# A two-layer hybrid block on one Trainium2 core: expert weights in 16 KB runs, the gather between the products, and a tiled input stage

## The reference

```python
def expert_choice_ffn(x, w_router, w_gate_up, w_down):      # x (1, 512, 1024), 16 experts, width 1024
    cap = EC_CAPACITY_FACTOR * T // N_EXPERTS                # 64 rows for each expert
    aff = jax.nn.softmax(jnp.einsum('btd,de->bte', x, w_router), axis=-1)
    gate, idx = lax.top_k(jnp.swapaxes(aff, 1, 2), cap)
    xs = x[bidx, idx]
    hg, hu = jnp.split(jnp.einsum('becd,edf->becf', xs, w_gate_up), 2, axis=-1)
    ye = jnp.einsum('becf,efd->becd', jax.nn.silu(hg) * hu, w_down)
    return jnp.zeros_like(x).at[bidx, idx].add(ye * gate[..., None])

# end of second_block
mix = jnp.einsum('bsd,de->bse', merged, w_out[l])
x = layer_norm(DN_ALPHA * x + mix, ln1_g[l], ln1_b[l])
ffn = expert_choice_ffn(x, w_router[l], w_gate_up[l], w_down[l])
x = layer_norm(DN_ALPHA * x + ffn, ln2_g[l], ln2_b[l])
```

## Time and profile before

| | |
|---|---|
| median of 3 runs (lowest, highest) | 2690.31 us (2686.57, 2691.11) |
| profiled execution, its span | 2694.53 us, 2692.5 us |
| TensorE busy | 2480.3 us, 92% of the span |
| VectorE (DVE) busy | 1105.0 us, 41% |
| ScalarE (ACT) busy | 813.3 us, 30% |
| GpSimd (POOL) busy | 168.9 us, 6% |
| DMA | 400.42 MB, mean 149 GB/s |
| chain that ended last | PE 80%, DVE 8%, DMA 5%, ACT 4% |

### The profile page before, as it was taken

How to read it: one execution, slowest core, us unless ns; L and a number is a source line. 1 busy time by engine, 2 the same in 40 slices (tenths; PEclk the granted TensorE clock), 3 DMA queues, 4 the chain that set the end, 5 groups by cost and what they waited for, 6 DMA issues and landing times.

```text
span 2692.5 us, 31030 instructions
## 1 busy us (share of the span) xinstructions
PE 2480.3 (92%) x13300; PEld 1829.3 (68%) x13300; DVE 1105.0 (41%) x1487; ACT 813.3 (30%) x1289; POOL 168.9 (6%) x156
## 2 busy tenths in 40 slices
PE   6999999999998999979999999987999879999996
PEld 4787788877776777867778878854778744444442
DVE  4747465343433323254334472657433621111113
ACT  5434544232323313142233343335422200000000
POOL 0102021111110000000000010210000000000000
PEclk9999999999998999989999999989999879999998
DMA  4122213232314223231222332331321279999995
GB/s 134 55 75 79 86 42 106 75 110 83 105 63 156 94 102 112 80 137 63 94 94 85 106 131 94 110 90 44 110 94 60 105 314 409 409 409 409 409 409 205
DMA packets 153800, 400.42 MB, mean 149 GB/s; under 512 B 7232, under 2 KB 25024, under 8 KB 153536
## 3 DMA queue, kind: packets, MB, share of 16 engines
q1 hardware_dynamic: 149504, 383.76, 38.3%
q0 software_dynamic: 4160, 14.68, 1.6%
HBM read 384.53 MB, written 13.89 MB: 148 GB/s over the span
## 4 chain that ended last, share of the span: by engine, by line
PE 80%; DVE 8%; DMA 5%; ACT 4%; issue 2%; SPq 0%; ACTq 0%; DVEq 0%
PE banks L94 19%; PE banks L96 18%; PE banks L95 18%; PE banks L1925 4%; PE banks L1956 4%; DMA work<-w_down_in 2%; PE banks L1906 2%; PE banks L1983 2%; DMA ring<-w_down_in 2%; DVE ring_split L88 1%; PE banks L1540 1%; PE banks L1438 1%; ACT halves_split L83 1%; DVE const L2421 1%; PE banks L1444 1%
## 5 line engine op out<-in xcount | busy, mean ns | idle before, releaser
L94 PE MATMUL banks<-work_split,ring_split 128*128 128x512 f32 x1536 | 625.2, 407 | 35.4 <-DVE ring_split L88 21.2
L88 DVE TENSOR_TENSOR ring_split<-ring,halves_split 128x1024 fp32r<-128x1024 f32 x284 | 355.6, 1266 | 680.0 <-ACT halves_split L83 679.9
L95 PE MATMUL banks<-work_split,halves_split 128*128 128x512 f32 x1536 | 605.8, 394 | 0.0
L96 PE MATMUL banks<-activations_T_split,halves_split 128*128 128x512 f32 x1184 | 468.0, 395 | 0.0
L83 ACT ACTIVATE halves_split<-ring 128x1024 fp32r<-128x1024 f32 x284 | 294.8, 1052 | 311.9 <-PE banks L96 258.7
L94 PEld LDWEIGHTS banks<-work_split,ring_split 128*128 128x128 f32 x1536 | 293.3, 191 | 108.3 <-DVE ring_split L88 24.9
L95 PEld LDWEIGHTS banks<-work_split,halves_split 128*128 128x128 f32 x1536 | 293.7, 191 | 58.6 <-issue 1.0
L96 PE MATMUL banks<-ring_split,work_split 128*128 128x512 f32 (+1 forms) x736 | 286.2, 389 | 0.0
L95 PE MATMUL banks<-halves_split,work_split 128*128 128x512 f32 x672 | 264.9, 394 | 0.0
L96 PEld LDWEIGHTS banks<-activations_T_split,halves_split 128*128 128x128 f32 x1184 | 225.9, 191 | 49.3
L94 PE MATMUL banks<-halves_split,work_split 128*128 128x512 f32 x384 | 153.7, 400 | 15.2 <-DVE ring_split L88 10.1
(11 more groups left out here) (319 smaller groups left out, 3124.6 us busy)
## 6 DMA issues: line engine op xcount, KB each, us to landing
ring<-w_in_in SPq DMA_DIRECT2D x31, 2048.0 KB, 7.8
ring<-w_gate_up_in SPq DMA_DIRECT2D x24, 2048.0 KB, 23.6
work<-w_gate_up_in SPq DMA_DIRECT2D x24, 2048.0 KB, 24.3
ring<-w_down_in SPq DMA_DIRECT2D x20, 2048.0 KB, 12.0
work<-w_down_in SPq DMA_DIRECT2D x12, 2048.0 KB, 18.8
ring<-w_in_in SPq DMA_DIRECT2D x17, 1024.0 KB, 7.8
ring<-w_up_in SPq DMA_DIRECT2D x8, 2048.0 KB, 7.8
halves<-w_gate_up_in SPq DMA_DIRECT2D x8, 2048.0 KB, 23.9
```

The source lines that it names most:

```text
L88: s.mark(dve.tensor_tensor(R(dst), src, R(hi).bitcast(F32), ALU.subtract), what)
L94: pe.matmul(out, R(ll), R(rh), start=start, stop=False)
L95: pe.matmul(out, R(lh), R(rh), start=False, stop=False)
L96: return pe.matmul(out, R(lh), R(rl), start=False, stop=stop)
```

## The change

Six things, in the order of the program:

1. *Input by tiles.* `x` is loaded in four quarters with a semaphore each; each tile is squared, its root taken and scaled on its own; the transposes run tile by tile; the 40-column product waits block by block, and the low halves of `AT` follow it pair by pair. A dummy root loads the table first.
2. *Out-projection.* Its weight loads are issued one step earlier for one half, the first three quarters of `mgT` and the first weight pieces are split within the end of the merge, and `tail_major` starts its first piece before the last block is merged.
3. *Norm and router.* The normalised rows are stored with permuted features (feature 8q+j at column 128j+q), ACT evacuates the transposes (DVE only the last), the logits are made transposed, tile by tile, with the router weight as the stationary side.
4. *Expert weights.* A load now takes, for each partition, one contiguous run of 16 KB (8 rows of the gate-and-up weight belong to a partition, a quarter load takes 2 of them over all 2048 columns; a down load takes 4 rows). `AT` is the last slot, the first three loads wait only for the end of the merge, and the first refill and the last pair come in halves.
5. *The round.* The gather of round p+1 and its gate transposes stand between gate/up and down of round p. The scatter multiplies an exact 0/1 matrix with a high and a low fp32r half of the gated rows, 16 one-pass products. Silu and the gate product wait for the whole of gate and up.
6. *The end.* In the last round the kept rows (`acc`) are put into the banks by a product with the identity, statistics are read from the banks, ACT applies the root from the banks, and GpSimd adds the second half of the bias row for three of the four tiles.

```diff
+        eslot = [slot5, slot6, ring[2], ring[0], ring[1], ring[3], slot4, AT]
+        scatter_banks = (0, 1, 6, 7, 3, 0, 1, 6)
+        scatter_after = (None, None, None, None, None, 0, 1, 2)
+        final_banks = (0, 1, 2, 6, 7, 3, 4, 5)
 # sync
-            ld_x.mark(sp.dma_start(XR, T["x"].rearrange("(t p) d -> p t d", p=P)), "x")
+            for t in range(NT):
+                ld_x[t].mark(sp.dma_start(XR[:, t, :], T["x"][t * P:(t + 1) * P, :]), "x")
...
-            WGU = T["w_gate_up_2"].rearrange("e (a k p) n -> e a p k n", p=P, a=2)
-            WDN = T["w_down_2"].rearrange("e (a k p) n -> e a p k n", p=P, a=2)
+            WGU = T["w_gate_up_2"].rearrange("e (p q k) n -> e q p (k n)", p=P, q=4)
+            WDN = T["w_down_2"].rearrange("e (a p k) n -> e a p (k n)", p=P, a=2)
...
+                        for h in range(2):
+                            sp.wait_ge(*e_pe(("half0.0", "group0.0")[h]))
+                            for e in range(2):
+                                load_half(e_w[(c + e) % ES], c + e, h, f"h{c + e}" if h == 0 else f"w{c + e}")
...
+                elif c < 3:
+                    sp.wait_ge(*mg_pe("br23.1"))
                 elif c < 7:
                     sp.wait_ge(*l_pe("m31"))
 # gpsimd
+            for t in range(NT - 1):
+                pool.wait_ge(*f_vec(f"mul{t}"))
+                f_pool.mark(pool.tensor_tensor(XR[:, t, 512:], acc[:, t, 512:], lnrow2[:, 1, 512:], ALU.add), f"x{t}")
 # scalar
+            for t in range(NT):
+                act.wait_ge(*ld_x[t]("x"))
+                n_act.link(act, act.activation(AT[:, 2 * t:2 * t + 2, :], XR[:, t, :].rearrange("p (a b) -> p a b", a=2), ACT.Square, accum_out=stat[:, t:t + 1]))
+                n_act.mark(act.activation(stat[:, 4 + t:5 + t], stat[:, t:t + 1], ACT.Sqrt, bias=eps, scale=1.0 / DM), f"rms{t}")
...
+                    e_act.mark(act.activation(R(ye_hi[:, n, :]), psum[4 + n][:, :], ACT.Copy, scale=gcol[:, p % 2:p % 2 + 1]), f"y{n}.{p}")
 # tensor
+            def logits(t):
+                for k in range(KB):
+                    mm = pe.matmul(psum[2 * t][0:NE, 0:P], wr[:, k, :], AT[:, k, t * P:(t + 1) * P], start=(k == 0), stop=(k == KB - 1))
...
+            def kept(n, t):
+                pe.matmul(psum[final_banks[4 * n + t]][:, :], ident, acc[:, t, n * 512:(n + 1) * 512], start=True, stop=False)
+            def scatter(p, n):
+                for t in range(NT):
+                    if not last and scatter_after[m] is not None:
+                        pe.wait_ge(*e_vec(f"acc{scatter_after[m]}.{p}"))
+                    pe.matmul(to, R(SPT[:, t * P:(t + 1) * P]), R(ye_hi[:, n, :]), start=not last, stop=False)
+                    e_pe.mark(pe.matmul(to, R(SPT[:, t * P:(t + 1) * P]), R(ye_lo[:, n, :]), start=False, stop=True), f"y{m}.{p}")
...
                     if p and q == 0:
-                        pe.wait_ge(*e_act(f"a1.{p - 1}"))
-                        pe.wait_ge(*e_act(f"y1.{p - 1}"))
+                        pe.wait_ge(*e_vec(f"acc4.{p - 1}"))
+                        pe.wait_ge(*e_vec(f"acc7.{p - 1}"))
+                        pe.wait_ge(*e_vec(f"yl1.{p - 1}"))
...
+                    gather(p + 1, range(5))
                 turn(0)
+                turn(1)
+                    gather(p + 1, range(5, KB))
+                    turn_gate(p + 1)
 # vector
-            dve.wait_ge(*s_pe("proj"))
-            for q in range(4):
+            def split_x(q):
+                dve.wait_ge(*s_pe(f"proj{q}" if q < 3 else "proj"))
                 dve.wait_ge(*n_act(f"ATh{q}"))
                 a = AT[:, 2 * q:2 * q + 2, :]
                 low(dve, n_vec, a, a, at_hi[:, 2 * q:2 * q + 2, :], f"ATl{q}")
...
+                    if c and g == 2 and part == "br":
+                        if b == 0:
+                            low_mg(0)
+                            low_mg(1)
+                        if b == 3:
+                            low_w(0)
+                            low_w(1)
...
-                vec_s.mark(dve.scalar_tensor_tensor(XR[:, t, :], v, stat[:, 8 + t:9 + t], rows[:, 1, :], ALU.mult, ALU.add), f"x{t}")
+                turned = lambda x: x.rearrange("p (q j) -> p q j", j=KB)
+                vec_s.mark(dve.scalar_tensor_tensor(XR[:, t, :].rearrange("p (j q) -> p q j", j=KB), turned(v), stat[:, 8 + t:9 + t], turned(rows[:, 1, :]),
+                                                    ALU.mult, ALU.add), f"x{t}")
...
+                    e_vec.mark(dve.scalar_tensor_tensor(R(ye_lo[:, n, :]), psum[4 + n][:, :], gcol[:, p % 2:p % 2 + 1], R(ye_hi[:, n, :]).bitcast(F32),
+                                                        ALU.mult, ALU.subtract), f"yl{n}.{p}")
+            def final_stats(t):
+                f_vec.link(dve, dve.bn_stats(fst[:, t, 6:12], psum[final_banks[4 + t]][:, :]))
+            def final_norm(t):
+                v, to = acc[:, t, :], 512 if t < NT - 1 else DM
+                f_vec.mark(dve.tensor_tensor(v, v, lnrow2[:, 0, :], ALU.mult), f"mul{t}")
+                f_vec.mark(dve.tensor_tensor(XR[:, t, 0:to], v[:, 0:to], lnrow2[:, 1, 0:to], ALU.add), f"x{t}")
```

More of the change, by code:

```diff
@@ L1288, in _, with high_mg, high_w @@
-            roots(l_act, l_vec)
+            def high_mg(n):
+                high(act, l_act, mg_hi[:, 2 * n:2 * n + 2, :], mgT[:, 2 * n:2 * n + 2, :], f"mg{n}")
+            def high_w(n):
+                high(act, l_act, l_rows[n % 4], out2_rows(n), f"w{n}")
+            act.wait_ge(*mg_vec("m23.0"))
+            high_mg(0)
+            high_mg(1)
+            for n in range(2):
+                act.wait_ge(*l_w[n]("w"))
+                high_w(n)
+            act.wait_ge(*mg_vec("m21.1"))
@@ new lines, in _, with root @@
+            high_mg(2)
+            act.wait_ge(*mg_pe("br21.1"))
+            high_w(2)
+            act.wait_ge(*mg_vec("m23.1"))
+            high_mg(3)
+            high_w(3)
+            for n in range(4, 8):
+                act.wait_ge(*l_pe(f"p{n - 4}"))
+                high_w(n)
+            def root(act_s, vec_s, t):
+                act.wait_ge(*vec_s(f"var{t}"))
+                act_s.mark(act.activation(stat[:, 8 + t:9 + t], stat[:, 2 * t + 1:2 * t + 2], ACT.Sqrt, bias=eps5), f"root{t}")
@@ new lines, in copy_x, with copy_logits @@
+            def copy_x(t, q):
+                act.wait_ge(*q_pe(f"T{t}{q}"))
+                q_act.mark(act.activation(AT[:, 4 * q:4 * q + 4, t * P:(t + 1) * P], psum[2 * t + q][:, :].rearrange("p (b c) -> p b c", b=4), ACT.Copy), f"AT{t}{q}")
+            def copy_logits(t):
+                act.wait_ge(*q_pe(f"logits{t}"))
+                q_act.mark(act.activation(lgT[0:NE, t * P:(t + 1) * P], psum[2 * t][0:NE, 0:P], ACT.Copy), f"logits{t}")
+            root(l_act, l_vec, 0)
+            root(l_act, l_vec, 1)
@@ L1289, in _ @@
+            copy_x(0, 0)
+            copy_x(0, 1)
+            root(l_act, l_vec, 2)
+            copy_x(1, 0)
+            copy_x(1, 1)
+            root(l_act, l_vec, 3)
+            copy_x(2, 0)
+            copy_x(2, 1)
+            copy_logits(0)
+            copy_logits(1)
+            copy_x(3, 0)
+            copy_logits(2)
+            copy_logits(3)
+            act.wait_ge(*q_vec("less"))
+            q_act.mark(act.activation(affN, affN, ACT.Exp), "exp")
             for t in range(NT):
@@ L1596, in _, with tail_major @@
                 merge(1, c)
-            def tail_major(vec_s, pe_s, hi, lo, view, between):
+            def tail_major(vec_s, pe_s, hi, lo, view, rows, between, second=None):
                 def step(n, t):
@@ L1608, in tail_major @@
                     pe.wait_ge(*vec_s(f"w{n}"))
+                    if n == 1 and second:
+                        second()
                     for t in range(NT):
@@ L1948, in turn @@
+                    mm = rows(q, 0)
+                    if p == 0 and q == 0:
+                        e_pe.mark(mm, "half0.0")
+                    e_pe.mark(rows(q, 1), f"group{q}.{p}")
                 def turn(f):
                     pe.wait_ge(*e_vec(f"ga{f}.{p}"))
+                    if p and f == 0:
+                        pe.wait_ge(*e_vec(f"acc3.{p - 1}"))
                     for b in range(4):
@@ L2613, in _ @@
                 experts(p)
[L2614 to L2616 removed]
+            final_norm(0)
+            final_inv(3)
+            for t in range(1, NT):
+                final_norm(t)
 def constants():
```

379 lines of the change are left out of this document (228 added, 151 removed).

## The result

The changed kernel takes 2645.4 us (median of 4 runs, 2643.6 to 2648.6) against 2690.7 for the kernel before beside it (4 runs, 2686.6 to 2693.4): 0.9834 of the time, 95% interval 0.9817 to 0.9851. Run again later on another occasion it took 2643.8 (5 runs, 2640.6 to 2648.7), 0.9822 [0.9809, 0.9836]. The forecast was 2644, the range 2630 to 2668. The medians are 45.3 apart.

A forecast was written before the change was run, and what follows sets the result against it. In the expert stage TensorE wants 58.4 us a round and DMA 61.5, limits 5% apart. Gains of 12 + 21 + 9.2 + 4 = 46 take the profiled 2694.5 to 2648.5, 4.2 above the median, so 2644; range 2630 to 2668.

The forecast's parts named there:

- The input stage: Start of the kernel: first split product at 24.4 for 39.06, group 2 at 39.3 for 52.5; gain 12, bounds 8 and 14.7.
- Out-projection, router, first gather: Between merge and experts: 6.4 + 1.2 + 10.0 + 4.0 = 21.6, less 0.6 for a cold gather: gain 21.
- between nothing and double I take nothing: Last pass of each norm, writing with a 512-byte stride: no extra time taken; double would be 5.1 in all.
- DVE's reduction of logits 18 us earlier: Router: a sign to look for in the trace, DVE reducing the logits 18 us earlier.
- The expert stage: First expert product to last down product: 470.0 before, 460.8 after, a gain of 9.2; TensorE's round 58.5, loads 59.2.
- The estimate of 416: Expert loads: GB/s by a fixed overhead of about 3 bus cycles a packet, 5.04 us a load; 425 was taken.
- the check on DMA: Expert stage: 439 to the loads' end, some 5 of stalls, 3.5 of products behind the last halves: 449, under 461.
- Rival B: Expert loads: the 16 KB pieces bring no rate, 409 GB/s stays; 4 us more, 2648; chance 0.17.
- D: Expert loads: pieces 64 KB apart make HBM reads slower; at 355 GB/s 27 slower, 2717; chance 0.05.
- C: Expert rounds: DVE is the bound at each scatter, 10 us instead of 8; 16 more, 2660; chance 0.13.
- E: Front gains given back: ACT's chain, DVE's strided passes and POOL at their bad ends; 13 more, 2657; chance 0.14.
- The tail: Last down product to end of span: 29.4 now, 25.4 after; gain 4, bounds 0 and 8.

The follow-up runs named there:

- experiment 1: Changed kernel with the input stage as in the kernel before (x in one load, one root, transposes block by block): 2657.2 us, 0.9864.
- experiment 12: The changed kernel itself, unaltered, timed again beside other runs on one chip: 2643.8 us.
- experiment 6: Changed kernel with the last pass of the norm ahead of the router writing without the 512-byte stride, features in old order: 2642.1 us, 0.9805.
- experiment 8: Changed kernel with the next round's gather put back behind the scatter, all eight blocks in one piece: 2670.8 us, 0.9904.
- experiment 4: Changed kernel with a lighter load stream alone, 2 MB less a round from the second round on, same TensorE work: 2646.2 us, 0.9816.
- the split wait: Changed kernel where a round's first product no longer waits for the eighth add, only the first product into bank 6 does; as experiment 3: 2643.4 us.
- the best version: Changed kernel with the split wait, second low half behind the second add, DVE alone adding tail bias rows; as experiment 10: 2635.7 us, 0.9789.
- experiment 2: Changed kernel with the expert loads in 4 KB pieces of the old layout, everything behind them as changed: 2658.5 us, 0.9873.
- experiment 3: Changed kernel with the eighth-add wait moved from a round's first product to the first product into bank 6: 2643.4 us, 0.9815.
- experiment 10: Changed kernel with the split wait, second low half made behind the second add, and DVE alone adding the tail's bias rows: 2635.7 us, 0.9789.
- Experiment 9: Changed kernel with DVE alone adding the bias rows of the tail, POOL doing nothing there: 2643.7 us, 0.9817.
- experiment 5: Changed kernel with the lighter load stream of experiment 4 and the split wait: 2638.0 us, 0.9788.

## Why the prediction was right, and where it was not

**The sum.** 46 was forecast. By the traces 48.2 came, by the medians 45.3; 2645.4 is 1.4 us above the forecast of 2644. In each of the four terms the mechanism that was forecast is the one that worked, but that the sum came so close is partly luck: one term was 3.6 too high, another 4.1 too low, and they offset each other.

**The input stage**: 11.7 for 12, shown by experiment 1 (the same kernel's second trace, of experiment 12, is some 1.8 us further ahead behind this stage). The two times on which it hung, 24.4 and 39.3, came at 24.60 and 38.53.

**Out-projection, router, first gather**: 17.4 for 21. The first out-projection product comes 5.1 us earlier beyond the input's 11.7, the idle that stood ahead of it. With the slow clock behind it gone too, the start of DVE's norms moved by 19.4 where 18.4 was forecast, the input stage included. The loss lies behind that. The step that failed is "between nothing and double I take nothing" for the strided pass: it takes 0.7 to 0.8 us more, four times, 3.1 (experiment 6). With the pass at double its time the prediction had this sum at 16; the pass takes 60% more, and the measured 17.4 lies between 16 and 21. The Trainium skill (SBUF — State Buffer, the note on cachelines) says that accesses which cross to a new 16-byte line pay, without a size, and the trace agrees. Second, DVE's reduction of the logits starts 7.1 us behind the start of the last transposes instead of 5.6. The prediction put one tile's logits there, 1.8 us; the program puts two, which took 5.3 at a granted clock of 0.71 (3.6 in experiment 12). Third, the first gather gives 2.3 (9.71 to 7.43) for 3.6, at a granted clock of 0.61. The sign "DVE's reduction of logits 18 us earlier" left the input stage out: by the prediction's own terms it was 29.6, and it came 26.3 earlier.

**The expert stage**: 13.3 for 9.2. The rate was forecast at 425 and is 428. The estimate of 416, worked out from the overhead that the Trainium skill gives for a packet (DMA: Bandwidth & Descriptors, Why small descriptors are slow), is too low: the measured step from 409 to 428 is over twice the step to 416. TensorE's round is 57.69 for 58.5: the hand-over 0.45 shorter, the middle (gather to the end of down, 22.5 us) 0.4 shorter. Six full rounds were forecast at 351.0 us and took 347.2: five of 57.69, and one of 58.73 in which the scatter's one-pass products ran 0.43 us apart. With the first and the last round within 0.1 us of their forecast, this is the 4 us. That the gather's move itself is worth over 2.4 us a round is shown by experiment 8, and that TensorE sets the round by experiment 4.

**The step that was wrong in kind** is the check on DMA: "and behind the last halves 3.5 of products: 449, under 461", a lead of 12 us. (Its terms add up to 447.8, not 449.) The first part held: from the first expert product to the last byte the terms give 444.3, and by the windows it is 444.0 in the changed kernel, 444.1 with the split wait, 442.0 in the best version. The last stretch with loads (length, clock, DMA share, GB/s) of the changed kernel, then of the best version; the 5 us ahead of each are full (share 1.01), so the loads end at 2608.0 and 2606.6:

```profile
2605.00:2610.00 5.00, 1.00 0.60 249
```

```profile
2605.00:2610.00 5.00, 1.00 0.32 133
```

But the down product ends 11.9 us behind the last byte in the best version, where the loads set the time, and 12.8 in the changed kernel. So the lead was not 12 us but about 1. With the gate and up pair as the critical load (experiment 2), and not the last halves, the check would have read 444.3 + 11.9 = 456 against 461. Rival B, "at 5.13, four more", would have read 474 against 461, that is 13: experiment 2 shows 13 by the medians, 17 by its trace. The range held B's true price only because it was wide for other reasons. It also hid what the change leaves on the table: with both limits 1 us a round apart, a further gain on TensorE alone passes only in part (experiments 3 and 10).

**The rivals.** B is out (428 GB/s, and 409 in the same kernel with 4 KB pieces, experiment 2). D is out (428 GB/s with pieces 64 KB apart). C is out: 7.55 us, and DVE is named for 3.3 of it. E is half seen: the strided pass came, ACT's chain and POOL did not.

**The tail**: 5.9 for 4. The first product of the norms starts 8.95 us behind the last down product (forecast 9.8). The four tiles take 11.3; the prediction allowed 12.6, though its own terms add up to 12.3. The end takes 3.3 (3.0). POOL's pass took 1.7 where 1.25 was assumed, but half of it is hidden. Experiment 9's trace shows that it should not be there.

## What to carry to other kernels

When two limits lie within a few per cent, price the load side by the landing on which the longest remaining work hangs, not by the last byte: here the pair four pieces ahead of the end, with 29 us of products behind it against 20 us of loads. Test it by making the stream lighter with the engine's work unchanged, and by relieving the engine with the stream unchanged: 0 and 2 us alone, 8 together. And look at the granted clock before a gain that stays away is put down to a wait: in experiments 3 and 5 several rounds stayed long by the clock alone. Of a change of layout, price the stride on each engine that could carry it; DVE's 3 us were the cheap place, TensorE's weight loads the dear one.

## What the runs showed of the hardware

- A piece of 16,384 bytes took 613 ns on its engine, one of 4,096 bytes 160 to 164 (8,192: 309), and the sum over the engines is 428 GB/s against 409; 64 KB between the pieces of neighbouring partitions (gate and up) cost nothing to be seen: the rate is the same 427 to 428 in every full slice, with the down pieces, which adjoin, among them.
- A DVE pass of 1,024 elements a partition went from 1.28 to 1.97 to 2.09 us when it wrote with a stride of 512 bytes. Four ACT copies that read with that stride took 7.43 us, and 3.88 when contiguous.
- A gather product whose stationary operand is read with a stride of 32 bytes took twice the time (weight load 192 to 335 ns, 40 records 4.66 to 9.71 us), while the router's transposes, which read the same tile with the same stride, stayed at 0.27 us each (their weight loads went from 140 to 191 ns).
- DVE's pass over SBUF of 1.22 us took 1.96 to 2.28 with a POOL pass of 1.70 to 1.77 beside it: together slower than DVE doing both, 2.4 us a tile for 2.93.
- Idle stretches of 1.9 us on TensorE were mostly followed by products at full pace (0.23 apart), but in one of the changed kernel's seven hand-overs by products 0.43 apart with a granted clock of 0.57 over 2568 to 2572, and behind four of the seven of experiment 5 by a granted clock down to 0.50. With the gather put back (experiment 8) the down products behind 1.93 us of idle began slower in every round (14.7 to 15.6 us for 13.88). What tells these cases apart, no run shows.
